# Differential-attention weights ahead of the splits, and tokens gathered for four experts at once in the rounded format

## The reference

```
h = rmsnorm(x, norm1_g)
c, vm, z, qd, kd, vd = split(h @ w_in)                 # 12 units of 256 columns
y_m = mlstm_group(c, vm, z, ...)                       # short convolution of c, 4 heads of 128
y_d = diff_attention(qd, kd, vd, lam, rel_bias)        # 4 heads, two softmaxes each, p0 - lam * p1
x = x + concat(y_m, rmsnorm(y_d)) @ w_out
t = rmsnorm(x, norm2_g)
# routing: one group of 4, then 2 of its 8 experts, for each token
for e in range(32):
    out += gates[:, e] * ((silu(t @ w_eg[e]) * (t @ w_eu[e])) @ w_ed[e])   # 1024 -> 512 -> 1024
x = x + out
```

## Time and profile before

| | us |
|---|---|
| median of 3 runs | 1888.15 (1884.62 to 1889.56) |
| the profiled execution | 1886.47 |
| its span, first to last instruction | 1884.3 |
| PE busy | 1805.2 (96%) |
| DVE busy | 942.5 (50%) |
| ACT busy | 727.7 (39%) |
| DMA, mean over the span | 228 GB/s |

### The profile page before, as it was taken

How to read it: one execution, slowest core, us unless ns; L and a number is a source line. 1 busy time by engine, 2 the same in 40 slices (tenths; PEclk the granted TensorE clock), 3 DMA queues, 4 the chain that set the end, 5 groups by cost and what they waited for, 6 DMA issues and landing times.

```text
span 1884.3 us, 25574 instructions
## 1 busy us (share of the span) xinstructions
PE 1805.2 (96%) x10262; PEld 1390.0 (74%) x10262; DVE 942.5 (50%) x1190; ACT 727.7 (39%) x964; POOL 41.4 (2%) x55
## 2 busy tenths in 40 slices
PE   8977999999999989999999999999999999999997
PEld 7776644544544468888987888778888999888886
DVE  6455211111111156566675656756566554665665
ACT  5453111111111154345555434654245445453444
POOL 2000000000000000000000000000000000200000
PEclk9988999999999999999999999999999999999999
DMA  8325889999999965555424555545555544455551
GB/s 279 101 76 202 335 343 422 422 423 420 423 422 421 422 218 180 195 182 170 135 90 151 183 196 180 179 141 192 180 198 166 177 154 151 164 190 183 188 191 56
DMA packets 191202, 428.71 MB, mean 228 GB/s; under 512 B 7292, under 2 KB 145632, under 8 KB 166560
## 3 DMA queue, kind: packets, MB, share of 16 engines
q1 hardware_dynamic: 187952, 418.41, 60.9%
q0 software_dynamic: 3184, 9.36, 1.5%
HBM read 426.69 MB, written 1.05 MB: 227 GB/s over the span
## 4 chain that ended last, share of the span: by engine, by line
PE 78%; DMA 8%; DVE 7%; ACT 5%; issue 1%; SPq 0%; DVEq 0%; POOL 0%; ACTq 0%
PE pw L475 55%; PE acc L475 22%; DMA mring<-in_w_eu 7%; DVE wl L1644 2%; ACT wh L1149 1%; ACT arena L1328 1%; PE pw L814 1%; DVE x L2082 0%; DMA raw<-in_w_in 0%; ACT sm L1320 0%; ACT arena L1434 0%; DVE scr L2094 0%; ACT L1179 0%; DVE arena L1707 0%; DMA cB<-in_decays 0%
## 5 line engine op out<-in xcount | busy, mean ns | idle before, releaser
L475 PE MATMUL pw<-aa,wh 128*128 128x512 f32 (+1 forms) x2512 | 704.2, 350 | 4.8 <-DVE aa L1672 3.2
L475 PE MATMUL pw<-aa,wl 128*128 128x256 f32 x1960 | 552.5, 282 | 0.0
L1644 DVE TENSOR_TENSOR wl<-raw,wh 128x2048 fp32r<-128x2048 f32 x205 | 463.5, 2298 | 174.4 <-ACT wh L1149 173.4
L475 PEld LDWEIGHTS pw<-aa,wh 128*128 128x128 f32 x2512 | 439.4, 191 | 76.7 <-issue 4.7
L1149 ACT ACTIVATE wh<-raw 128x2048 fp32r<-128x2048 f32 x205 | 381.4, 1905 | 25.6 <-DMA raw<-in_w_in 7.8
L475 PEld LDWEIGHTS pw<-aa,wl 128*128 128x128 f32 x1960 | 373.0, 190 | 1.5
L475 PE MATMUL acc<-wh,aa 128*128 128x512 f32 x1088 | 351.5, 397 | 15.2 <-DVE wl L1644 5.8
L475 PE MATMUL pw<-mring,arena 128*64 128x512 f32 x1536 | 338.4, 595 | 7.5 <-DMA mring<-in_w_eu 6.6
L475 PEld LDWEIGHTS pw<-mring,arena 128*64 128x64 f32 x1536 | 108.6, 137 | 210.5 <-issue 206.9
L475 PEld LDWEIGHTS acc<-wh,aa 128*128 128x128 f32 x1088 | 207.4, 191 | 63.3 <-DVE wl L1644 6.0
L475 PE MATMUL acc<-wl,aa 128*128 128x512 f32 x544 | 214.7, 395 | 0.0
(11 more groups left out here) (400 smaller groups left out, 1315.7 us busy)
## 6 DMA issues: line engine op xcount, KB each, us to landing
raw<-in_ffn_w_in SPq DMA_DIRECT2D x88, 1024.0 KB, 5.1
mring<-in_w_eg SPq DMA_DIRECT2D x64, 1024.0 KB, 17.3
mring<-in_w_eu SPq DMA_DIRECT2D x64, 1024.0 KB, 19.3
mring<-in_w_ed SPq DMA_DIRECT2D x64, 1024.0 KB, 18.0
raw<-in_ffn_w_out SPq DMA_DIRECT2D x44, 1024.0 KB, 5.0
raw<-in_odd_w_in SPq DMA_DIRECT2D x24, 1024.0 KB, 5.2
raw<-in_w_in SPq DMA_DIRECT2D x12, 1024.0 KB, 10.8
raw<-in_even_w_in SPq DMA_DIRECT2D x11, 1024.0 KB, 5.5
```

The source lines that it names most:

```text
L475: return pe.matmul(out, lhs, rhs, start=start, stop=stop, skip_group_check=True)
L1644: dve.tensor_tensor(wl[:, u % RING, :], raw[:, u % RING, :], wh[:, u % RING, :].bitcast(F32), ALU.subtract).then_inc(sig(f"{ep}_lo"), 1)
```

## The change

In the first block, `diff_weights(h)` moves ahead of the next `split` on DVE, `bias_rows()` ahead of splits 4 and 5, `head_rstd` ahead of split 14, and splits 14 and 15 ahead of the last copies. In the router, `masks` are computed ahead of the gates, and the two runs of zero products get shorter. The experts go by quads: `sel` covers 4 experts in fp32r, the tokens are split into `h2_hi` (by ACT) and `h2_lo` (by POOL, in place of `h2`), and one gather of 4 parts, 32 fp32r products with 256 moving columns, serves two pairs. The order of unit loads on SP is the same.

```diff
@@ gpsimd, behind gain(a["normf_g"], 0)
+            for t in range(NT):
+                w.more("h2_high")
+                pool.tensor_tensor(h2_lo[:, t, :], h2[:, t, :, :].rearrange("p k f -> p (k f)"),
+                                   h2_hi[:, t, :].bitcast(F32), ALU.subtract).then_inc(sig("h2_low"), 1)
@@ tensor
-            keep_clock(32, pw[:, 3, :])
+            keep_clock(17, pw[:, 3, :])
...
-            keep_clock(30, pw[:, 3, :])
+            keep_clock(22, pw[:, 3, :])
...
-            def gather(half):
-                for k in range(4):
+            def gather(part):
+                for kk in range(2):
+                    k = 2 * part + kk
                     for t in range(NT):
-                        last = mm(pw[:, 2 + half, k * P:(k + 1) * P], h2[:, t, 4 * half + k, :],
-                                  sel[:, t, :, :].rearrange("p e s -> p (e s)"), t == 0, t == 1)
-                last.then_inc(sig(("gathered_low", "gathered")[half]), 1)
+                        for h, rows_ in enumerate((h2_hi, h2_lo)):
+                            last = mm(pw[:, 2 + part % 2, kk * T:(kk + 1) * T], rows_[:, t, k * P:(k + 1) * P],
+                                      sel[:, t, :], t == 0 and h == 0, t == 1 and h == 1)
+                last.then_inc(sig("gathered"), 1)
...
+            def quad(z):
+                a_, b_ = z * 2, z * 2 + 1
...
+                gate_up(1, a_, 0)
+                if behind:
+                    scatter(1)
+                pe.wait_ge(sig("gu_ready"), a_ * 2 + 2)
+                pe.wait_ge(sig("hid_ready"), a_ * 2 + 1)
+                turn_gated(1)
+                slots_turned(a_, 0)
+                pe.wait_ge(sig("hid_ready"), a_ * 2 + 2)
+                down(a_)
...
+                gate_up(1, b_, 1)
+                pe.wait_ge(sig("hid_ready"), b_ * 2 + 1)
+                pe.wait_ge(sig("sel_ready"), z + 2)
                 gather(0)
-                pe.wait_ge(sig("gu_ready"), i * 2 + 2)
+                pe.wait_ge(sig("gu_ready"), b_ * 2 + 2)
                 turn_gated(1)
-                pe.wait_ge(sig("selT_ready"), i + 1)
+                pe.wait_ge(sig("selT_ready"), b_ + 1)
                 gather(1)
+                pe.wait_ge(sig("xg_low"), z * 2 + 3)
+                gather(2)
+                pe.wait_ge(sig("xg_high"), z * 2 + 3)
+                gather(3)
+                pe.wait_ge(sig("hid_ready"), b_ * 2 + 2)
+                down(b_)
@@ scalar
+            split("a", 15)
             w.more("heads_turned", 2)
             w.more("lam")
             for h in range(NH):
                 act.activation(ah[:, 12 + h, :], pw[:, h // 2, (h % 2) * T:(h % 2 + 1) * T], ACT.Copy,
                                scale=sm[:, 93:94]).then_inc(sig("high"), 1)
-            split("a", 15)
...
+            for t in range(NT):
+                act.activation(h2_hi[:, t, :], h2[:, t, :, :].rearrange("p k f -> p (k f)"), ACT.Copy).then_inc(sig("h2_high"), 1)
@@ vector
-            for p in range(1, 5):
+            for p in range(1, 4):
                 split("a", p)
             convolution()
...
-            split("a", 5)
             bias_rows()
-            split("a", 6)
+            for p in range(4, 7):
+                split("a", p)
...
+            diff_weights(0)
             split("a", 9)
-            diff_weights(0)
...
+            split("a", 14)
+            split("a", 15)
             w.more("heads_turned")
...
-            split("a", 15)
```

More of the change, by code:

```diff
@@ L831, in down, with scatter @@
                                     last.then_inc(sig("m_used"), 1)
-            def scatter(final=False):
-                for t in range(NT):
[L836 to L845, removed]
+            def scatter(t, final=False):
+                for half in range(2):
+                    for y in (y_hi, y_lo):
+                        last = mm(acc[:, 2 * t + half, :], selT[:, t * P:(t + 1) * P], y[:, half * 512:(half + 1) * 512], False, False)
+                if final:
+                    last.then_inc(sig("scattered"), 1)
@@ L1363, in pair, with quad @@
                     act.activation(y_hi[:, half * 512:(half + 1) * 512], pw[:, 1 - half, :], ACT.Copy, scale=slot_gate).then_inc(sig("y_high"), 1)
[L1365 to L1367 removed]
+            def quad(z):
+                pair(z * 2)
+                pair(z * 2 + 1, z)
+            quad(0)
+            with act.Fori(0, nr * QUADS + (QUADS - 1)) as q:
+                quad(q + 1)
             act.wait_ge(sig("m_used"), nr * (PAIRS * PU) + PAIRS * PU)
@@ L1973, in _, with in_group @@
             dve.sem_inc(sig("dve_result"), 1)
+            def in_group(val, dst):
+                for t in range(NT):
+                    g4 = ghot[:, t, :].unsqueeze(2).broadcast_to([P, 4, 8])
+                    dve.tensor_tensor(dst[:, t, 0:32].rearrange("p (g j) -> p g j", g=4), g4,
+                                      val[:, t, :].unsqueeze(1).broadcast_to([P, 4, 8]), ALU.mult).then_inc(sig("dve_step"), 1)
+                w.more("dve_step", 2)
+            both = r3(240, 8)
+            then(dve.tensor_tensor(both, hot1, hot2, ALU.add))
+            in_group(both, masks)
+            dve.sem_inc(sig("masks"), 1)
             w.more("act_result", 2)
@@ L1981, in _ @@
             then(dve.tensor_tensor(rt[:, 232:234], rt[:, 230:232], rt[:, 82:84], ALU.mult))
-            both = r3(240, 8)
-            then(dve.tensor_tensor(both, hot1, hot2, ALU.add))
-            then(dve.tensor_tensor(hot1, hot1, wide(rt[:, 230:232], 8), ALU.mult))
-            then(dve.tensor_tensor(hot2, hot2, wide(rt[:, 232:234], 8), ALU.mult))
-            then(dve.tensor_tensor(hot1, hot1, hot2, ALU.add))
-            for t in range(NT):
-                g4 = ghot[:, t, :].unsqueeze(2).broadcast_to([P, 4, 8])
-                for val, dst in ((both, masks), (hot1, gate_all)):
-                    dve.tensor_tensor(dst[:, t, 0:32].rearrange("p (g j) -> p g j", g=4), g4,
-                                      val[:, t, :].unsqueeze(1).broadcast_to([P, 4, 8]), ALU.mult).then_inc(sig("dve_step"), 1)
-            w.more("dve_step", 4)
-            dve.sem_inc(sig("masks"), 1)
             w.more("psum_for_dve")
```

154 lines of the change are left out of this document (93 added, 61 removed).

## The result

The changed kernel takes 1858.95 us (median of 4 runs, 1855.63 to 1862.12), the kernel before beside it 1888.11 (4 runs, 1884.62 to 1889.56): the ratio is 0.985, with a 95% interval of 0.9834 to 0.9865. Forecast was 1857.5, in a range of 1849 to 1869. The profiled execution of the changed kernel took 1862.12 us, the longest of its four, with a span of 1860.1; PE is busy 1771.1 us.

The account below looks back on a forecast made before the run. Waits of PE were taken to cost time ahead of the experts, loads at 422 GB/s to bound the experts. Terms 7.4 + 12.9 + 5.9 + 2.4 + 0 + 2.2 - 0.2 = 30.6 us, from 1888.15 to 1857.5 us; range 1849 to 1869.

Parts of the forecast that it names:

- First block, start: Query and key products: PE no longer waits for the bias row and keeps full clock; 7.4 us gained, bounds 4.7 and 7.7.
- Heads 0 to 3: Four heads of the first block: attention weights ready earlier, PE waits less for DVE; 12.9 us gained.
- ACT takes it back: Rival: at each head PE waits for ACT instead of DVE; heads give 7 us, total gain 20, 1868; chance 0.15.
- Last rows: `last_rows`: wait for split 15 falls from 5.83 to 1.85 us and the clock stays up; 5.9 us, bounds 4.0 and 6.1.
- Zero products: Ahead of the tokens' transposes: 17 zero products instead of 32 end sooner; 2.4 us gained, 0 if the clock falls.
- Router and first gather: Earlier masks worth 1.8 us net, cancelled by POOL's subtractions holding up DVE 1.8 us; 0, bounds +1.8 and -3.
- A clock of 0.50 between 160 and 190: Sign against the forecast: PE at half clock around the router, in the rival that doubles about 10 us of PE work.
- Pair 0: First expert pair: no gather inside it, so pair 1's slots are released earlier; 2.2 us gained, bounds 0 and 2.7.
- fixed stream of loads: Experts: after pair 1's slots are released, loads at 422 GB/s set the time; PE's later savings are worth nothing.
- The loop: Expert pairs: PE per pair falls from 28.2 to about 26.7 us, but loads still take 29.8; no gain, tail -0.2 us.

Follow-up runs that it names:

- all but the first block: Changed kernel with the first block in its old order, router and experts kept as changed; 1882.05 us, ratio 0.9977 to the kernel before.
- the first block's order alone: Kernel before with only the first block's DVE and ACT moves, router and experts as before; 1859.08 us, ratio 0.9863.
- the low part on DVE: Changed kernel with the two `h2_lo` subtractions on DVE instead of POOL, ahead of its wait for the logits; 1857.48 us, ratio 0.9853.

## Why the prediction was right, and where it was not

The mechanism was the forecast's: the waits of PE in the first block went, the loads kept the pace in the experts. That the total came within 1.5 us is in part luck. The profiled spans differ by 24.2 us, 6.4 less than the sum of 30.6 (that execution is the changed kernel's longest of four); the medians differ by 29.2. Two terms, the last rows and pair 0, gave less than forecast in that execution, and the second block took 2.6 us more.

- **First block, start** (7.4): 7.3 in the trace, 8.1 alone. No wait, and the products ran at 2.4 GHz in 3.62 us where 3.5 was forecast.
- **Heads 0 to 3** (12.9): 14.2 in the trace, 12.3 by the ratios of the experiment that undoes them. (The bounds that the prediction names for it, below 7 and above 14.5, are wider than the -3 and +1.6 that its own range uses.) ACT's copy takes 1.74 us at head 1 where 1.9 was forecast. The rival *ACT takes it back* gave 7 for this part; it fell, since the new waits for ACT (1.6 to 1.7 us) are not as long as the old ones for DVE (2.43 to 6.17), and the next heads' weights come late by 0.15 and 1.71 us only. Only the experiment that put ACT's copy first showed why ACT's order is no free gain: its split is what DVE waits for next.
- **Last rows** (5.9): the term was mis-sized, 3.7. The wait fell to 2.01 us as forecast (1.85), but in this execution the clock did not stay up behind it, 146 to 148 us at 0.50. Where it did, `last_rows` took 1.6 us less. The result lies just under the term's lower bound of 4.0; the term took as certain what happened in five of seven profiled executions.
- **Zero products** (2.4): 2.5, and putting them back cost 3.0 in the trace together with the second run.
- **Router and first gather** (0): -0.7. The hold-up of DVE by POOL is there, 1.2 us where 1.8 was forecast, and POOL's 2.36 us each stood against 2.5. What was not forecast: behind PE's wait for the masks, 1.66 us, the clock was 0.54 (178 to 180 us), and the first seven gather products come 0.21 us apart instead of 0.12. A clock of 0.50 between 160 and 190 was named as a sign of a wrong step; it came, for 3 us and not for 10.
- **Pair 0** (2.2): -0.2 in the changed kernel's execution; in five others 2.1 us are there at the last wait for a unit. The release came 2.35 us earlier in every execution with the new gather, 25.0 against 27.35. From the first experts' product to the end of the experts it was 463.6 us against 463.4 before, so here it was worth nothing. The step in question is "the time until pair 1's slots are released at 241.92, plus a fixed stream of loads". From pair 1's first release to PE's last wait for a unit it is 430.5 us before and 430.3 after. What the loads moved in that time, first before, then with the change (stretches of the two traces; last three columns clock, DMA share, GB/s):

```profile
214.57:241.92 27.35, 1.00 0.76 307
241.92:267.00 25.08, 1.00 0.96 369
267.00:615.00 348.00, 1.00 1.01 422
615.00:645.05 30.05, 1.00 1.01 421
```

```profile
187.56:212.57 25.01, 1.00 0.83 336
212.57:240.00 27.43, 1.00 0.94 367
240.00:588.00 348.00, 1.00 1.01 422
588.00:617.88 29.88, 1.00 1.01 422
```

  That is 307 x 27.35 + 369 x 25.08 + 422 x 348 + 421 x 30.05 = 177.2 MB before, and 336 x 25.01 + 367 x 27.43 + 422 x 348 + 422 x 29.88 = 177.9 MB after (with the products in thousands). The unit that PE waits for last is the same in both (the second up unit of the last pair's first expert), so 0.8 MB more, 1.8 us of the stream, had gone into units behind it.

  But this is not so in every execution. The experiment with the zero products back has the changed kernel's experts:

```profile
188.67:213.68 25.01, 1.00 0.84 336
213.68:240.00 26.32, 1.00 0.95 366
240.00:588.00 348.00, 1.00 1.01 422
588.00:617.08 29.08, 1.00 1.02 423
```

  These are 177.2 MB, as before the change, and 428.4 us: 2.1 us were gained. Leaving out the gather issued twice, eight profiled executions have the new gather: five took 428.2 to 428.4 us for this stretch, with 177.1 to 177.2 MB moved, and three (the changed kernel's, all but the first block, the heads' weights behind the splits) 429.6 to 430.3, with 177.4 to 177.9 MB. The three with the old gather took 430.0 to 430.8. So the fixed stream was right in five executions: from pair 2's release to the last wait they took 403.2 to 403.4 us, the old ones 402.7 to 403.4. In the other three the needed unit came 1.3 to 2.0 us later, with 0.3 to 0.8 MB more (0.7 to 1.8 us of the stream) moved for units behind it. That it shares the 422 GB/s with them and is late by this is argued from these sums; no run changed the depth of the queue alone. What decides which of the two happens stays open; the five lie in the later groups of runs, in which no kernel with the old gather was profiled. Behind the last wait 0.3 us are lost (29.6 instead of 29.25; -0.2 was forecast), and in three executions another 0.7 to 1.5 by the clock. From the first experts' product to the end of the experts it is 461.6 to 463.6 us in the eight and 462.9 to 463.7 in the three.
- **The loop** (0): right. 422 GB/s, PE's waits for units 23.8 us instead of 6.6. Of 30 us of added PE work 23 disappeared in them. The whole change of the gather, from float32 per pair to rounded per quad, bought little: all but the first block gave 3.5 us, of which the shorter zero products are 2.5. No run changed the gather alone.
- **Second block**: 2.6 us longer in the profiled execution, though the change does not touch it. The same wait of 2.0 us stands near the end of both kernels; before, the clock stayed at 1.00 behind it, after, it fell to 0.57 from 1828 to 1832, which made that stretch 1.7 us longer. The other 0.9 us are not traced. Over the twelve profiled executions this block, which no experiment touches, took 1207.0 to 1213.0 us, so differences of a few us between two spans say nothing of the part that was changed. The changed kernel's median lies 3.2 us below its profiled run.
- **Signs named in advance**: query and key products at 40 (40.21), under 1 us ahead of head 1's transposes (0.64) and near 2 behind them by ACT (1.74), the end of `last_rows` near 156 (157.00), the first experts' product near 182 (183.91), loads at 422 GB/s (421 from 500 to 634 us) and more waits for `mring` (20 instead of 5) came. Longer ones did not: the longest is 1.3 us before and after.

## What to carry to other kernels

Where a matrix engine waits for a short operation that stands behind a long one in a list written by hand, the order of the two is worth more than any faster form of the work: 26.5 of 29.2 us came from it. When the next wait belongs to another engine, moving its list too can put a long operation behind a copy that waits, for no gain at all (ACT's copies here). In a stage whose loads run at their full rate, less work does not move the end: 23 of 30 us of added work disappeared. An earlier release moves it at most by its own size, here by 2.1 us of 2.35 in five executions and by 0.2 to 0.9 in three: measure from the first release to the last wait, and in more than one execution.

## What the runs showed of the hardware

- The same wait of PE is followed by a lower granted clock in some executions and not in others. Ahead of `last_rows` (2.01 us) it fell in 2 of 7 profiled executions (12.8 against 11.1 to 11.2 us). Near the kernel's end (2.0 us) the clock was 0.57 to 0.63 in a stretch of 4 us behind it in 4 executions, and 1.00 in 8. At the end of the experts (2.26 us) it was 0.57 to 0.65 in the 4 us behind the wait in 3 executions, and 1.00 in 9.
- The granted clock falls under a PE that has work without a gap. Behind the router's 32 records of 36 columns, the zero products ran at 0.65 to 0.80 in seven of the nine executions with the changed router, and at 1.00 in the other two (the changed kernel's own among them) and in all three with the router of before. What sets it there stays open.
- A fall of the clock costs nothing where another engine is late anyway. The first rows of `w_out` took 11.2 us in three executions (the first block's order alone, the low part on DVE, the gather twice) and 12.3 to 13.1 in the others, the changed kernel's with 12.8 among them. In the three the clock had fallen one wait earlier, to 0.50 from 118 to 120 us, and PE reached head 3 later, with a wait of 0.17 to 0.20 us for DVE's weights; in the changed kernel's it was 1.00 there, PE waited 1.71, and the clock fell in the rows:

```profile
126.21 0.52 PE L644 MATMUL pw<-cA,scr 128*128 128x128 f32 x3 [0.20 <-DVEq L1798]
```

  The row is from the first block's order alone. The rows of `w_out` ended at 140.0 to 140.2 us in the three and at 141.3 in the changed kernel.
- POOL's two-input subtraction of 128x1024 takes 2.36 us, twice DVE's 1.18, and holds up a DVE instruction of 0.17 us until it ends (1.03 to 1.39 us in six executions).
